# Merge's gate projections placed in the differential attention and the head norms, the recurrence's gates placed among projection tiles, and another order of the expert capacities

## What is computed

```
def diff_attend(q, k, v, lam):                 # 8 heads, 2 maps a head, 256 queries, 512 keys
    s = einsum('bhmqd,bhmkd->bhmqk', q, k) * DH_D ** -0.5
    p = softmax(s, axis=-1)
    a = p[:, :, 0] - lam * p[:, :, 1]
    return einsum('bhqk,bhkd->bhqd', a, v)

def merge_branches(p, a_out, b_out, w_a, w_b, w_o):   # p[8], p[9]: two projections of u
    y = sigmoid(p[8]) * (a_out @ w_a) + sigmoid(p[9]) * (b_out @ w_b)
    return y @ w_o

# mixture of experts: 32 experts, the 4 best of each token, 256 tokens
    act = h_glu * sigmoid(SWIGLU_ALPHA * h_glu) * (h_lin + 1)
    return act @ w2[e] + b2[e]

# recurrence of the second block, per channel
    r, i = sigmoid(gate_a(xc)), sigmoid(gate_x(xc))
    a = exp(-C * softplus(lam) * r)
    h[t] = a * h[t - 1] + sqrt(1 - a ** 2) * i * xc[t]
    mixed = gelu(gate) * h
```

## Time and profile before

| | us |
|---|---|
| median of the runs | 2896.99 (of 2896.99, 2896.99, 2903.4) |
| the profiled execution | 2903.46 |
| its span in the trace | 2901.6 |
| TensorE busy | 2517.1 (87%) |
| VectorE busy | 768.3 (26%) |
| ScalarE busy | 552.0 (19%) |
| DMA, mean over the span | 210 GB/s, 608.35 MB |

### The profile page before, as it was taken

One profiled execution on the slowest core, in us unless ns is written; L12 is line 12 of the kernel. 1 busy time (PEld: TensorE's weight loads), 2 busy tenths in 40 slices (PEclk: granted clock), 3 DMA queues, 4 the chain that ended last, 5 costly groups with the idle time before them and its releaser, 6 DMA issues. The chain is left out here.

```text
span 2901.6 us, 36397 instructions
## 1 busy us (share of the span) xinstructions
PE 2517.1 (87%) x15176; PEld 1647.3 (57%) x15176; DVE 768.3 (26%) x1863; ACT 552.0 (19%) x1358; POOL 16.3 (1%) x25
## 2 busy tenths in 40 slices
PE   3999976779899898887868776989999999999998
PEld 1785743468634334332323223767887788667876
DVE  1010046621211111211101112670541325624421
ACT  2110111500212111111111112351211211412110
POOL 0000000000000000000000000000000000100000
PEclk7899997889799999989999897989999999999999
DMA  6222231025276999999999996313333334113432
GB/s 268 70 104 102 101 146 58 0 95 230 87 324 264 421 421 420 420 420 421 421 421 421 421 420 252 121 68 116 116 136 120 131 136 145 44 73 116 145 114 75
DMA packets 88101, 608.35 MB, mean 210 GB/s; under 512 B 10560, under 2 KB 12992, under 8 KB 17248
## 3 DMA queue, kind: packets, MB, share of 16 engines
q1 hardware_dynamic: 84752, 599.82, 52.2%
q10 hardware_dynamic: 3088, 5.78, 0.5%
q0 software_dynamic: 96, 0.39, 0.0%
HBM read 604.91 MB, written 1.05 MB: 209 GB/s over the span
## 5 line engine op out<-in xcount | busy, mean ns | idle before, releaser
L495 PE MATMUL bank<-arena,ring 128*128 128x272 f32 (+2 forms) x3456 | 826.1, 402 | 19.5 <-DVEq L559 18.4
L495 PEld LDWEIGHTS bank<-arena,ring 128*128 128x128 f32 x3456 | 658.9, 191 | 181.8 <-issue 45.9
L2137 PE MATMUL bank<-arena 128*32 128x512 f32 x2304 | 286.9, 620 | 50.1 <-DMA arena<-in_w_e 49.9
L521 PE MATMUL bank<-arena,ring 128*128 128x272 f32 x1216 | 287.7, 396 | 6.1 <-DVE arena L1640 6.1
L521 PEld LDWEIGHTS bank<-arena,ring 128*128 128x128 f32 x1216 | 233.0, 192 | 56.7 <-DVE arena L1640 7.0
L1516 DVE TENSOR_TENSOR arena<-bank,arena 128x256 f32<-128x256 f32 x56 | 23.8, 424 | 841.1 <-PE bank L2116 841.1
L2137 PE MATMUL bank<-ring,arena 128*32 128x512 f32 x1280 | 172.6, 654 | 41.4 <-DMA ring<-in_w_e 41.1
L2137 PEld LDWEIGHTS bank<-arena 128*32 128x32 f32 x2304 | 64.4, 111 | 216.4 <-DMA arena<-in_w_e 109.5
L2154 PE MATMUL bank<-arena 128*32 128x256 f32 x1760 | 118.8, 412 | 43.7 <-DMA arena<-in_w_e 39.7
L1626 DVE SCALAR_TENSOR_TENSOR arena<-arena,par 128x272 f32<-128x272 f32 x296 | 148.5, 502 | 10.5
L2154 PE MATMUL bank<-ring,arena 128*32 128x256 f32 x1824 | 115.0, 398 | 28.8 <-DMA ring<-in_w_e 25.5
(11 more groups left out here) (381 smaller groups left out, 2124.4 us busy)
## 6 DMA issues: line engine op xcount, KB each, us to landing
arena<-in_w_e SPq DMA_DIRECT2D x224, 1024.0 KB, 26.0
ring<-in_w_e SPq DMA_DIRECT2D x160, 1024.0 KB, 26.2
ring<-in_w_up SPq DMA_DIRECT2D x44, 1024.0 KB, 4.8
ring<-in_w_l SPq DMA_DIRECT2D x37, 1024.0 KB, 4.8
ring<-in_w_ada SPq DMA_DIRECT2D x24, 1024.0 KB, 6.2
ring<-in_w_proj SPq DMA_DIRECT2D x24, 1024.0 KB, 4.7
ring<-in_w_down SPq DMA_DIRECT2D x32, 704.0 KB, 4.0
ring<-in_w_merge SPq DMA_DIRECT2D x16, 1024.0 KB, 4.7
```

The costliest lines, as they stand in the source:

```text
L495: mm = pe.matmul(o[:, 0:n], ring[:, s, k * 256 + c * P:k * 256 + (c + 1) * P], rhs(k), start=(k == 0), stop=(k == KT - 1))
L521: mm = pe.matmul(o[:, 0:n], ring[:, s, k * P:(k + 1) * P], rhs(part * kt + k), start=(part == 0 and k == 0), stop=(part == parts - 1 and k ...
L2137: mm = pe.matmul(bank[q * GROUP:(q + 1) * GROUP, 4 + g % 2, :], xe[:, (g // CHUNK) % 2, k, s:s + GROUP], w[:, q * 512:(q + 1) * 512], star ...
```

## The change

- **Merge.** The eight units of the two gate projections come first in the stream, then branch a and branch b in turns. Their 16 tiles (`gate_tile` on TensorE, `gate_copy` on ScalarE) go: tiles 0 to 3 ahead of the attention, tiles 4 to 11 one into each head, tile 12 behind phase 3's arrival, tiles 13 to 15 behind the sums of the norm of `bout`. They are copied without the sigmoid to the unused context half of `u` and to `gb` (the place of `og`); the 16 sigmoids follow in a row when the last tile is copied. Tiles 4 to 13 use bank 7 alone, and the value products of the attention bank 6 alone. TensorE only arrives at phases 2, 3 and 4 (`arrive`); it waits for phases 2 and 3 later, and for phase 4 not at all.
- **Norms and lambda.** The reciprocal of the norm of `bout` is taken tile by tile, with a count `bout_normed` for each. Lambda's products, sum and exponential move ahead of phase 2.
- **Full rows.** `d_scores` reads two zero-padded copies of `qd` that GpSimd makes behind phase 1, so a matmul has 128 rows; `m_rows` has 128 rows too, of which 124 are zero.
- **Experts.** The same capacities in another order. The arena slot at 11264 becomes the last of the 14 slots and opens at `merged`.
- **Recurrence.** `lru_gates` go singly behind projection tiles. VectorE's small operations on lambda follow the convolutions. GpSimd takes two products (L1688 and L1696 before). The root moves on ScalarE behind the copies of K and V.

The diff, cut:

```diff
-CAPACITY = [3, 1, 5, 1, 1, 4, 1, 1, 4, 1, 1, 3, 1, 3, 1] + [2, 1] * 8 + [1]
+CAPACITY = [3, 1, 2, 1, 3, 1, 2, 1, 4, 1, 2, 1, 1, 5, 1, 1, 2, 1, 4, 1, 2, 1, 3, 1, 2, 1, 2, 1, 1, 2, 1, 1]
...
+        def gate_bank(n):
+            alone = 4 <= n <= 13
+            return bank[:, 7 if alone or n % 2 else 6, 0:T], alone
...
+            def gate_copy(n):
+                free = tile_out(act, at, n % 2 == 1)[1]
+                act.activation(u[:, n, T:2 * T] if n < 8 else gb[:, n - 8, :], gate_bank(n)[0], ACT.Copy).then_inc(free, 1)
+            for n in range(3):
+                gate_copy(n)
+            phase(act, 2)
+            gate_copy(3)
...
             phase(act, 3)
             act.wait_ge(sem("bout_ready"), NH_D)
             norm_squares(act, lambda k: bout[:, k, :], lambda k: sq8[:, k, :])
+            gate_copy(12)
...
             phase(act, 4)
+            for n in range(13, 16):
+                gate_copy(n)
...
+            for n in range(8):
+                act.activation(u[:, n, T:2 * T], u[:, n, T:2 * T], ACT.Sigmoid).then_inc(sem("gate_sig"), 1)
+                act.activation(gb[:, n, :], gb[:, n, :], ACT.Sigmoid).then_inc(sem("gate_sig"), 1)
...
             dve.wait_ge(sem("head_root"), 2)
-            chain(dve.reciprocal(rs8[:, :, :], rs8[:, :, :]))
             for k in range(KT):
-                ins = dve.scalar_tensor_tensor(out=bout[:, k, :], in0=bout[:, k, :], scalar=dg[:, k:k + 1],
-                                               in1=rs8[:, k, :], op0=ALU.mult, op1=ALU.mult)
+                chain(dve.reciprocal(rs8[:, k, :], rs8[:, k, :]))
+                dve.scalar_tensor_tensor(out=bout[:, k, :], in0=bout[:, k, :], scalar=dg[:, k:k + 1],
+                                         in1=rs8[:, k, :], op0=ALU.mult, op1=ALU.mult).then_inc(sem("bout_normed"), 1)
             phase(dve, 4)
...
             def lru_scan(n):
+                dve.wait_ge(sem("lru_gated"), n + 1)
                 chain(dve.tensor_tensor(xc[:, n, :], xc[:, n, :], th[:, n, :], ALU.mult))
-                chain(dve.tensor_tensor_scan(out=ig[:, n, :], data0=rg[:, n, :], data1=xc[:, n, :], initial=0.0,
-                                             op0=ALU.mult, op1=ALU.add))
-                dve.wait_ge(sem("lru_gelu"), n + 1)
-                dve.tensor_tensor(mix[:, n, :], ga[:, n, :], ig[:, n, :], ALU.mult).then_inc(sem("lru_mixed"), 1)
+                dve.tensor_tensor_scan(out=ig[:, n, :], data0=rg[:, n, :], data1=xc[:, n, :], initial=0.0,
+                                       op0=ALU.mult, op1=ALU.add).then_inc(sem("lru_scanned"), 1)
...
+            for n in range(8):
+                pool.wait_ge(sem("lru_scanned"), n + 1)
+                pool.wait_ge(sem("lru_gelu"), n + 1)
+                pool.tensor_tensor(mix[:, n, :], ga[:, n, :], ig[:, n, :], ALU.mult).then_inc(sem("lru_mixed"), 1)
...
+            def gate_tile(n):
+                s = slot_filled(pe, at)
+                o, alone = gate_bank(n)
+                last = at.out - 1 if alone else at.out - 2
+                pe.wait_ge(sem(f"bank_read{last % NL}"), last // NL + 1)
...
             for h in range(NH_D):
                 if h < NH_D - 1:
                     d_scores(h + 1)
+                gate_tile(4 + h)
...
-            phase(pe, 4)
+            arrive(pe)
+            for n in range(13, 16):
+                gate_tile(n)
             for p in range(4):
-                project(pe, at, 1, u_lat, T)
                 project(pe, at, 1, lambda k: aout[:, k, :], T)
-                project(pe, at, 1, u_lat, T)
-                project(pe, at, 1, lambda k: bout[:, k, :], T)
+                project(pe, at, 1, lambda k: bout[:, k, :], T, first=lambda k: pe.wait_ge(sem("bout_normed"), k + 1))
```

More of the change, by code:

```diff
@@ L278, in lay_out @@
     w1 = i["l1_w_in_2"]
[L279 removed]
+    merge = [units(i["w_branch_a"][0]), units(i["w_branch_b"][0])]
     out = {
@@ L497, in project @@
                     mm.then_inc(sem("tile_done") if c == 0 else sem("unit_used"), 1)
+                    if behind is not None:
+                        behind(2 * unit + c)
                 at.unit += 1
@@ L614, in program @@
         sq8 = take(KT, T, at=work + 2048)
-        sg = take(2, T, at=work)
+        qz = [arena[:, a:a + NH_D * T].rearrange("p (a b) -> p a b", a=NH_D)
+              for a in (vm_at - 4 * 2 * T, vm_at + KT * T)]
+        gb = og
         tmg = take(T, at=work + 512)
@@ L1850, in _ @@
         def _(pool):
-            for n in range(1, 5):
+            phase(pool, 1)
+            for m in range(2):
+                pool.memset(qz[m][64 * (1 - m):64 * (2 - m), :, :], 0.0)
+                pool.tensor_copy(qz[m][64 * m:64 * m + 64, :, :], qd[64 * m:64 * m + 64, :, :])
+            for n in range(2, 5):
                 phase(pool, n)
@@ L1995, in d_scores @@
                         pe.wait_ge(sem("probs"), 4 * h + j - 3)
-                    pe.matmul(bank[:, j, :], qd[64 * m:64 * m + 64, h, qt * P:(qt + 1) * P],
-                              kd[64 * m:64 * m + 64, h, :], start=True, stop=True).then_inc(sem("scores"), 1)
+                    pe.matmul(bank[:, j, :], qz[m][:, h, qt * P:(qt + 1) * P], kd[:, h, :],
+                              start=True, stop=True).then_inc(sem("scores"), 1)
             d_scores(0)
@@ L2318, in lru_gates @@
                   .then_inc(sem("lru_gates"), 1)
-            for half in range(2):
-                project(pe, at, 1, ub_k, L)
-                for n in range(4 * half, 4 * half + 4):
-                    lru_gates(n)
-            project(pe, at, 2, ub_k, L)
+            pre_unit()
+            pe.wait_ge(sem("lru_loaded"), 16)
+            project(pe, at, 3, ub_k, L, first=ub_first, behind=lambda c: lru_gates(c - 1) if c >= 1 else None)
+            at.ub += KT
+            project(pe, at, 4, ub_k, L, behind=lambda c: lru_gates(c + 5) if c < 3 else None)
             s = slot_filled(pe, at)
```

141 lines of the change are left out of this document (78 added, 63 removed).

## The result

| | before | after |
|---|---|---|
| median of the runs | 2897.26 us | 2847.3 us |
| range of the runs | 2896.99 to 2903.4 | 2845.61 to 2851.41 |
| span of the profiled execution | 2901.6 | 2845.7 |
| ratio, with its 95% interval | | 0.9825 (0.9808 to 0.9842) |

The account below looks back on a forecast made before the run. Dependent VectorE and ScalarE chains were taken to bound 493 to 600 us, elsewhere mostly TensorE or DMA; -42.3 - 12 - 1 = -55.3 from 2903.46 gave 2848.2, lowered by 6.5 to 2842, range 2826 to 2858.

Parts of the forecast that it names:

- Four tiles before the attention, nothing charged: Merge: four gate tiles ahead of the differential attention are hidden; GpSimd's fills and copies charged nothing, up to 3 us in range.
- The cycle of a head, 9.25: Differential attention: one gate tile in each head lengthens its cycle from 7.0 to 9.25 us, +2.25 for 3.45 of work.
- The new wait at tile 15: Merge's last gate tiles: TensorE stands 13 us before tile 15, as ScalarE's copy of tile 13 waits for phase 4.
- The rival without it (2828): Merge: the stop at tile 15 is absent or short, 13 us less, 2828; chance 0.10.
- the Merge term: Moving sixteen gate tiles ahead, into and behind the attention ends Merge at 670.9 instead of 713.24 us: -42.3 us.
- Capacities, -12: Experts: the new order shortens the transfer hole at the 5-group expert from 26.5 to 13.7 us: -12, bounds -5 and -18.
- Recurrence, -1 (bounds -5 and +5): VectorE's eight scans: product moved to GpSimd gives -3.2, slower two-input products beside GpSimd +2.4: -1 us.
- I take no gain there: Recurrence: ScalarE's root in the new order waits for the V tile, ended at about the same time; no gain.
- lower clock after TensorE's longer wait: Recurrence: a possible lower TensorE clock after a longer wait, included in the bounds -5 and +5.
- Full rows, 0 (bounds -3 and +1): Scores with 128 rows instead of 64, row spread with 128 instead of 4: same columns, no time by themselves.
- The step from 2848.2 to 2842: Whole kernel: forecast set below the 2848.2 sum because the median of before lies 6.5 us below its profiled execution.
- The clock rival (0.05): From 493 to 600 us TensorE's clock stays at half, outweighing all gains: 2919, slower than before; chance 0.05.

Follow-up runs that it names:

- the run on a single half: Changed kernel with 64-row scores, all four score matmuls of a head reading rows 0 to 63: 2849.12 us against 2847.3 of the changed kernel.
- the run with early copies: Changed kernel with ScalarE arriving at phase 4 behind its copies of gate tiles 13 to 15 and the sigmoids: 2837.41 us against 2847.3.
- Merge alone: Kernel before with only the Merge part of the change: 2865.02 us, ratio 0.9887, against 2897.65 us of the kernel before in these runs.

## Why the prediction was right, and where its steps were wrong

**Four tiles before the attention, nothing charged: right.** Scores start 14.3 us behind the end of the ada turns; forecast 13.9. GpSimd's four instructions take 7.4 us in all and end at 487.5, well ahead of the first scores.

**The cycle of a head, 9.25: the step that failed.** It stands in the forecast as "scores take 2.06", and again in the part on full rows: "have the same number of columns: no time by themselves". The row of before was of matmuls on two halves of the rows, which overlap; the changed ones can't, and take 3.60. That is 10.49 instead of 9.25, from the second cycle on, and 9.40 instead of 8.5 for the first: 8.3 us. The run with 64 rows gave 9.25 and, for the first, 9.14, so the scores are 7.7 of the 8.3 and the first cycle was reckoned 0.6 too short besides; the run on a single half gave 3.70 us for the scores. A count of columns was the wrong reason for a zero, and the 64*128 of the scores in the earlier trace rows was there to be read. The bound of +1 was too narrow.

**The new wait at tile 15: right**, 12.87 against 13, through the chain that was named (tile 13's bank, ScalarE's copy, the phase, eight reciprocals). The rival without it (2828) is what the run with early copies makes of it: one line moved takes 9.9 us off. The eight norms take 17.5 us, forecast 17.1. Counted from the eighth reciprocal, root and start of tile 15 come within 0.3 us of the forecast and Merge's end 1.3 late, most of it tile 15 itself (6.34 us instead of 5.4). Together with 8.8 us from the ada turns to that reciprocal, this is the 10 us by which the Merge term was missed.

**Capacities, -12: right** in mechanism, place and length: hole 13.3 against 13.7, and 12.6 us back when undone (10.7 as a ratio to the kernel before of that group). That it agrees to half a microsecond is luck, since the stage moves by 3.5 us without an edit.

**Recurrence, -1 (bounds -5 and +5): mis-sized.** From its first product with the root to its first mask VectorE takes 11.8 us instead of 13.2, a gain of 1.4 where I had 0.8. But 1.0 of it is in the first scan (1.12 us to the next product instead of 2.11), where VectorE no longer waits 0.55 us for ScalarE's gelu, which I had left out. The other seven take 1.53 us each instead of 1.59: what leaves with the product nearly comes back in the scan, which takes 1.17 us beside a product on GpSimd and 0.72 alone. "I take no gain there" for the root was wrong by 1.4 us. TensorE starts the V tokens 62.35 us behind the first projection, and 63.89 in the kernel before and with the part undone; among the gates it stood 0.92 us there for ScalarE, and that stop is gone. The 8.6 us for which it stood behind the V tokens I had left out too, but they aren't on the way to the first mask. The "lower clock after TensorE's longer wait" is there: from the first turned mask to a stop of 2.90 us near the last ones the changed kernel takes 46.57 us, and the run with the part undone 45.32. But from there to the output projection it takes 9.55 instead of 12.61, so the sign of the whole was wrong. The nine executions of the new order take 5 to 8 us less from the norm sums to the end than those three of the old one, and 3 to 4 less than Merge alone; 2.8 is the order, the rest clock.

The Trainium skill, SBUF — State Buffer, Who interferes with whom, has VectorE and GpSimd share one pair of ports to SBUF under an exclusive lock, for which a VectorE instruction with two SBUF inputs contends with a GpSimd one that reads SBUF. The prediction's +3 by it took a whole GpSimd product for each scan. Here a product that started 0.28 us before the scan and takes 0.88 cost it 0.45, where 0.60 was left of it; so the trace shows a wait of the kind that the rule gives for a late start, somewhat shorter. The profile's times on GpSimd are too rough to hold the 0.15 against the rule.

**Full rows, 0 (bounds -3 and +1): wrong in both halves,** 8 us more in the scores, and 3.6 less by the medians (1.2 to 3.8 by the traces) in the row spread.

**The step from 2848.2 to 2842 was wrong.** I took off 6.5 because the profiled execution of before lay so far above its median. The changed kernel's four runs don't have that gap: its profiled one took 2847.5, its median 2847.3. The sum itself, 2848.2, was 0.7 off the profiled execution, by the cancelling, which is luck: +10 in Merge, +0.6 from there to the first expert, -4.5 ahead of Merge, -0.5 among the experts, -6.3 behind them.

**The clock rival (0.05) didn't come:** 1.00 in the heads.

## What to carry to other kernels

Moving work into a stretch that waits pays its full length only up to the point where that stretch's own cycle is reached, so sum the cycle engine by engine, and take the duration of each instruction for the shape that it will have, not for the one it had. An engine that copies for TensorE should arrive at a phase behind its copies, not ahead of them: one line was worth 10 us. Where a stage is bound by transfers, look for the times when none runs and shorten the longest hold of the buffers, and then sum all such times again, since a gain at the start can come back as a stop at the end. Before a few microseconds are put down to an edit, see how much its stretch moves between runs that don't edit it.

## What the runs showed of the hardware

Float32 matmuls of 64 rows and 512 columns on different halves of the rows overlap almost fully, also where the kernel issues two on one half and then two on the other: 2.06 us for four of them, 3.70 on one half, 3.60 with 128 rows. A contraction of 4 rows is not shorter than one of 128 (1.12 against 1.02 us for two records), and with it the clock behind the same stop is lower (6.69 against 5.30 us for the same 16 records). A few microseconds of granted clock move from one stretch to another when only the time of arrival changes, with no instruction edited there: in nine runs 21.8 to 22.0 or 23.8 to 23.9 us in one stretch go with 939 or 937 us in a later one, and the whole stays within 1.5 us.
